# Delta rule's inverse: one whole-array product for two heads, one turn per level, heads kept in their row half

## The chip, the cores and the metric

The kernel runs on one core of a Trainium2 chip as a single launch. The metric is the device time of one execution in microseconds (us). In float32 code each matmul of the program appears in the trace as two matmul records and two weight loads; a transpose through the matrix engine appears as one of each.

## The reference, cut to what matters

The program is a two-layer diffusion block over 256 context and 1024 latent tokens. Its first layer mixes tokens with an mLSTM and an RWKV-7 delta rule. The delta rule is the part of this case:

```python
def rwkv_scan(inputs, S):
    def step(S, xs):
        r, v, kk, w, k, a = xs
        sa = jnp.einsum('bhvk,bhk->bhv', S, -kk)
        S = S * w[:, :, None, :] + sa[..., None] * (kk * a)[:, :, None, :] + v[..., None] * k[:, :, None, :]
        return S, jnp.einsum('bhvk,bhk->bhv', S, r)
```

There are 8 heads of 64 columns, 1280 tokens and two directions. The kernel takes chunks of 64 tokens. Inside a chunk the steps depend on each other through a 64x64 strictly triangular matrix per head, and the chunk is solved with the inverse of (identity minus that matrix). This case is about how the inverse is built.

## The kernel before, in words

The stage is `stage_rwkv_scan` (from line 1540). There are 20 chunks and 2 directions, so 40 scan steps `s`; two steps (two `lane`s) form one batch `b`, and there are B = 20 batches. The 8 heads lie as J = 4 pairs; of pair `j`, head `q` = 0 has rows 0 to 63 and head `q` = 1 has rows 64 to 127. A batch thus has 16 inverses of 64x64.

The inverse is built by doubling. Level 0 is made by GpSimd (`begin_inverse`, line 1990). Then come TOP = 5 levels, n = 1 to 5, so 100 levels in the stage. A level is a chain over three engines:

- `half_product` (line 1833, TensorE) multiplies the strict matrix `strict_t` (the stationary side) with the 32 changed columns of `inv`. There are 16 products with a 64x64 block, and they go over all four combinations of row half and column half of the array (`quarters`).
- `copy_half` (line 1903, ScalarE) copies the result from PSUM into `half`.
- `turn_inverse` (lines 2047 and 2049, VectorE) writes the turned `inv` into `lower`, in three instructions, beside the half product.
- `upper_product` (line 1842, TensorE) multiplies `lower` with `half`: again 16 products of 64x64 over all four combinations.
- `merge_upper` (line 2055, VectorE) writes the result into `inv` under a mask. The next level's half product and turn wait for it.

So that the two products use all four combinations, `inv` stores the heads in two sets: set 0 holds the heads whose inverse lies in its own order and set 1 the others, `own_inverse` finds a head, and the result of a product changes the row half between steps. The PSUM results lie in two banks, `PAIR` and `PAIR + 1` (`pair_bank`, `pair_banks`).

The order on each engine is written out by hand, in the loops over `b` at the end of each engine's block. Between the two products of a level TensorE does work of the batch before (`begin_chunk` 1789, `solve_chunk` 1798, `begin_outputs` 1807, `update` 1815, `end_outputs` 1821) and of the batch ahead (`strict_products` 1732, `products` 1743), and `pull` 1780, `turn_keys` 1755, `turn_v` 1770. VectorE does `read_products` 2039, `add_rest` 2064 and `update_state` 2072 and 2073 between its turns; ScalarE copies `strict_t` (line 1934) and other results. Of these the matrix engine's blocks are: 1732, 1780, 1789, 1798 and 1807 are 64x64; 1743 is 64 rows by 128 columns; 1815 and 1821 are 128 rows by 64 columns; 1755 and 1770 are the whole 128x128. Lines 1732, 1789 and 1798 keep a head in its row half: head 0 uses rows and columns 0 to 63 of the array, head 1 rows and columns 64 to 127.

Of the kernel before, what the change touches and what calls it, by code (L numbers as in the profile page):

```python
# [1539 lines left out]
def stage_rwkv_scan(p, arena, operands, v_dram, shared, spare, own, chunk_decay, y, next_weights, free, bonus_dram):  # L1540
# [30 lines left out]
    strict_read = p.semaphore("r_strict_read")  # L1571
    level0_ready = p.semaphore("r_level0_ready")
# [23 lines left out]
    with ExitStack() as local:  # L1596
# [4 lines left out]
        strict_t = sb("strict_t", [P, 2, 2, J, C])  # L1601
        inv = sb("inv", [P, 2, 2, 2, J // 2, C])
        lower = sb("lower", [P, 2, J, C])
        half = sb("half", [P, 2, J, C // 2])
# [16 lines left out]
        identity = column(0, 5 + R_LEVELS).unsqueeze(1).broadcast_to([P, 2, J // 2, C])  # L1621
# [6 lines left out]
        fours = [(lane, jj) for lane in range(2) for jj in range(J // 2)]  # L1628
        quarters = [(0, 0), (1, 1), (0, 1), (1, 0)]
        four = lambda lane, jj: lane * (J // 2) + jj  # L1630
        own_inverse = lambda b, lane, j, q: inv[part(q), b % 2, (j % 2) ^ q, lane, j // 2, :]
        pair_bank = lambda which, lane, jj: bank(PAIR + which)[:, four(lane, jj) * P:four(lane, jj) * P + C // 2]
        pair_banks = p.psum[:, PAIR:PAIR + 2, :].rearrange("p r (f n) -> p (r f) n", n=P)[:, :, 0:C // 2]
        with nc.Block() as block:
# [88 lines left out]
            def _(pe):  # L1723
# [174 lines left out]
            def _(act):  # L1898
                def copy_half(b, n):
# [3 lines left out]
                    nc.scalar.copy(half[:, :, :, :].rearrange("p q f n -> p (q f) n"), pair_banks).then_inc(half_copied, 1)  # L1903
# [25 lines left out]
                def copy_strict(b, lane):  # L1929
# [4 lines left out]
                    nc.scalar.copy(strict_t[:, b % 2, lane], narrow(bank(STRICT)[:, lane * HALF:(lane + 1) * HALF])).then_inc(strict_read, 1)  # L1934
# [44 lines left out]
            def _(pool):  # L1979
                begun, added = [0], [0]  # L1980

                def begin_inverse(b, lane, q):
# [6 lines left out]
                    pairs = prod[part(q), b % 2, lane, q, :, part(q)].rearrange("p (j r) n -> p r j n", r=2)  # L1989
                    nc.gpsimd.tensor_tensor(inv[part(q), b % 2, :, lane], pairs if q == 0 else pairs[:, ::-1],  # L1990
# [12 lines left out]

                pool.wait_ge(masks_loaded, 16)
# [21 lines left out]
            def _(dve):  # L2026
# [14 lines left out]
                def turn_inverse(b, n):  # L2041
# [4 lines left out]
                    here = inv[:, b % 2].rearrange("p s l j n -> p s (l j) n")  # L2046
# [1909 lines left out]
```

## Time and profile before

| | us |
|---|---|
| median of 3 runs | 2453.71 |
| lowest and highest | 2449.43, 2456.01 |
| the profiled execution | 2456.63 |
| its span | 2454.8 |
| TensorE busy in the span | 2294.7 |
| VectorE busy | 1320.0 |
| ScalarE busy | 794.4 |
| GpSimd busy | 251.0 |

The span is the time between the first and the last instruction; 1.8 us of the execution lie around it. Busy time is the union of an engine's records. The matrix engine has two rows, PE for matmuls and PEld for weight loads, which overlap. PEclk is the clock granted to the matrix engine as a share of 2.4 GHz (0.50 is 1.2 GHz). A line of the timeline merges neighbouring instructions of one group: its first number is when the first began, the second how long until the last ended.

### The profile page before, as it was taken

What the parts mean: (1) busy time and instruction counts of PE and PEld (TensorE: products, weight loads), DVE (VectorE), ACT (ScalarE), POOL (GpSimd) and SP (SyncE); (2) the same over time, 40 slices, a digit from 0 to 9 for tenths busy, and PEclk for the clock granted to TensorE, in tenths of its full rate; (3) what the DMA queues carried; (4) which work ended last, traced back from release to release, by engine and by line L of the source; (5) the groups of instructions that cost most, each with busy time, mean ns of one, the idle gap of its engine ahead of it and who ended that gap; (6) DMA issues with size and microseconds to landing.
All of it is one profiled execution on the core that took longest, in us unless ns stands there. A gap on an engine that the chain in (4) does not pass through costs nothing. (4 is left out here: it accounts for less than half of the span.)

```text
span 2454.8 us, 50670 instructions
## 1 busy us (share of the span) xinstructions
PE 2294.7 (93%) x22140; PEld 1417.6 (58%) x22140; DVE 1320.0 (54%) x2181; ACT 794.4 (32%) x1533; POOL 251.0 (10%) x280
## 2 busy tenths in 40 slices
PE   6999999999989988888887998999998999999898
PEld 4444456666644447887784443444685666756443
DVE  3320335553348756777774454555395666667514
ACT  4121222224455653443232222110101445465411
POOL 0000000000002211111221102341100000000000
PEclk8999999999989998999999998999999999999999
DMA  8100122122056654433325422111122100000233
GB/s 332 60 19 7 43 78 76 63 66 73 19 154 145 172 155 112 118 94 95 90 61 196 138 98 76 47 47 34 69 104 80 36 27 27 28 18 10 96 97 117
DMA packets 131866, 207.29 MB, mean 84 GB/s; under 512 B 15629, under 2 KB 95245, under 8 KB 128062
## 3 DMA queue, kind: packets, MB, share of 16 engines
q1 hardware_dynamic: 118398, 154.74, 20.2%
q0 software_dynamic: 13248, 49.32, 7.0%
q8 instruction: 175, 2.87, 0.5%
q14 instruction: 45, 0.37, 0.1%
HBM read 154.01 MB, written 50.01 MB: 83 GB/s over the span
## 5 line engine op out<-in xcount | busy, mean ns | idle before, releaser
L737 PE MATMUL psum<-arena,shared 128*128 128x512 f32 (+1 forms) x864 | 328.3, 524 | 1.5 <-PEq L223 1.5
L2861 PE MATMUL psum<-arena,second_shared 128*128 128x512 f32 (+1 forms) x640 | 282.3, 568 | 11.1 <-PEq L3682 6.4
L737 PEld LDWEIGHTS psum<-arena,shared 128*128 128x128 f32 x864 | 156.9, 191 | 108.5 <-issue 101.5
L2861 PEld LDWEIGHTS psum<-arena,second_shared 128*128 128x128 f32 x640 | 112.4, 195 | 77.0 <-issue 71.8
L1243 PE MATMUL psum<-shared,arena 128*128 128x512 f32 x320 | 150.0, 618 | 0.0
L2247 PE MATMUL psum<-shared,fin_mix 128*128 128x512 f32 x320 | 143.4, 601 | 2.9 <-POOL fin_mix L2380 2.9
L2247 PEld LDWEIGHTS psum<-shared,fin_mix 128*128 128x128 f32 x320 | 59.8, 192 | 75.0 <-issue 71.5
L1243 PEld LDWEIGHTS psum<-shared,arena 128*128 128x128 f32 x320 | 60.3, 196 | 73.3 <-issue 72.9
L841 ACT ACTIVATE shared<-psum 128x512 f32<-128x512 f32 (+1 forms) x48 | 25.2, 525 | 216.2 <-PE psum L737 216.2
L1842 PE MATMUL psum<-r_half,r_lower 64*64 64x32 f32 x3200 | 78.6, 225 | 13.5 <-issue 11.2
L1903 ACT COPY r_half<-psum 128x256 f32<-128x256 f32 x100 | 37.3, 373 | 162.0 <-PE psum L1833 161.7
L2049 DVE STREAM_TRANSPOSE r_lower<-r_inv 64x256 f32<-64x256 f32 x200 | 87.9, 440 | 2.7
L1990 POOL TENSOR_TENSOR r_inv<-r_prod,shared 64x256 f32<-64x256 f32 x80 | 58.0, 724 | 291.2 <-PE psum L1798 184.2
L1833 PE MATMUL psum<-r_inv,r_strict_t 64*64 64x32 f32 x3200 | 73.9, 225 | 14.6 <-issue 10.9
L330 PE MATMUL psum<-arena,shared 128*128 128x512 f32 (+3 forms) x240 | 87.4, 523 | 0.0
L3146 DVE TENSOR_TENSOR arena<-arena,g_k 128x512 f32<-128x512 f32 x56 | 39.6, 706 | 87.4 <-ACT arena L3014 87.4
L3014 ACT ACTIVATE arena<-arena 128x1024 f32<-128x1024 f32 x64 | 69.4, 1084 | 34.6 <-DVE arena L3127 32.8
L2852 PE MATMUL psum<-second_shared,arena 128*128 128x128 f32 x640 | 80.3, 277 | 0.0
L1833 PEld LDWEIGHTS psum<-r_inv,r_strict_t 64*64 64x64 f32 x3200 | 61.5, 138 | 27.1 <-issue 16.9
L1842 PEld LDWEIGHTS psum<-r_half,r_lower 64*64 64x64 f32 x3200 | 65.9, 139 | 18.7 <-issue 13.0
L2055 DVE COPY_PREDICATED r_inv<-shared,psum 128x256 f32<-128x256 uint32 x100 | 49.6, 496 | 50.2 <-PE psum L1842 49.0
L2852 PEld LDWEIGHTS psum<-second_shared,arena 128*128 128x128 f32 x640 | 75.1, 192 | 1.1 <-issue 0.5
(457 smaller groups left out, 4257.6 us busy)
## 6 DMA issues: line engine op xcount, KB each, us to landing
arena<-scratch_operands SPq DMA_DIRECT2D x152, 128.0 KB, 2.7
shared<-in_l_w_in SPq DMA_DIRECT2D x22, 512.0 KB, 4.0
scratch_spill<-shared POOLq DMA_DIRECT2D x16, 640.0 KB, 3.2
second_shared<-in_l_w_in SPq DMA_DIRECT2D x20, 512.0 KB, 3.9
scratch_operands<-arena POOLq DMA_DIRECT2D x14, 640.0 KB, 8.3
scratch_operands<-arena POOLq DMA_DIRECT2D x28, 320.0 KB, 11.3
shared<-in_l_mod_w SPq DMA_DIRECT2D x8, 1024.0 KB, 9.4
t_matrix<-in_transform SPq DMA_DIRECT2D x8, 1024.0 KB, 4.9
```

The lines of the kernel that those rows point to most:

```text
L330: last = nc.tensor.matmul(p.psum[0:rows_out, bank_of[u], 0:width], lhsT, rhs, start=(k == 0), stop=(k == KT - 1))
L737: last = nc.tensor.matmul(p.psum[:, FILL + f % BANKS, 0:width], weight[:, q % PIECES, k, :], hT[:, k, at:at + width], start=(k == 0), stop ...
L1243: last = nc.tensor.matmul(p.psum[:, PROJECT + u % 2, :], hT[:, k, t * P:(t + 1) * P], weight[:, job, k, :], start=(k == 0), stop=(k == KT ...
L1833: last = nc.tensor.matmul(pair_bank(q, lane, jj)[part(r)], strict_t[part(q), b % 2, lane, 2 * jj + r, :], changed(own_inverse(b, lane, 2 * ...
L1842: last = nc.tensor.matmul(pair_bank(q ^ r, lane, jj)[part(q)], lower[part(r), q ^ r, four(lane, jj), :], half[part(r), q, four(lane, jj), ...
L1990: nc.gpsimd.tensor_tensor(inv[part(q), b % 2, :, lane], pairs if q == 0 else pairs[:, ::-1], identity[part(q)], ALU.add).then_inc(level0_r ...
L2049: last = nc.vector.transpose(lower[part(1 - q), 1], here[part(q), 1])
L2055: nc.vector.copy_predicated(whole[:, :, :, 1 - direction(b)], added_to_pairs(direction(b), n), pair_banks.rearrange("p f (g w) -> p f g w" ...
L2247: last = nc.tensor.matmul(p.psum[:, OUT + 2 * (t % 2) + n, :], mixed[:, t % SLOTS, k, :], weight[:, k, n * BANK:(n + 1) * BANK], start=(k ...
L2852: last = nc.tensor.matmul(bank[:, (t - part[0]) * P:(t - part[0] + 1) * P], hT[:, kk, t * P:(t + 1) * P], w[:, kk, :], start=(kk == 0), st ...
L2861: last = nc.tensor.matmul(bank[:, 0:width], w[:, kk, :], hT[:, kk, first:first + width], start=(kk == 0), stop=(kk == KT - 1))
L3014: nc.scalar.activation(out, out, ACT.Exp).then_inc(sig["exps_ready"], 1)
```

## The change

The strict matrices of the two heads of a pair are stored as one 128x128 block, one head in the upper left, the other in the lower right, with zeros in the other two quarters. The half product of a pair is then one matmul with this whole block (8 per level in place of 16), and each head stays in its own row half. The upper product has as many matmuls as before, but each uses rows and columns of its own half. `inv` has no sets any more, the turn is one VectorE instruction over 512 elements per partition, and both products lie in one PSUM bank. ScalarE copies a strict matrix in two instructions, one per row half. GpSimd clears the zero quarters once, at the start of the stage, in two instructions, and TensorE waits for these before its first product.

```diff
-        strict_t = sb("strict_t", [P, 2, 2, J, C])
-        inv = sb("inv", [P, 2, 2, 2, J // 2, C])
+        strict_t = sb("strict_t", [P, 2, 2, J, P])
+        inv = sb("inv", [P, 2, 2, J, C])
...
+        heads = [(lane, j) for lane in range(2) for j in range(J)]
+        own_inverse = lambda b, lane, j, q: inv[part(q), b % 2, lane, j, :]
+        narrowed = lambda where, lane, j: slice(where * HALF + (lane * J + j) * C // 2, where * HALF + (lane * J + j + 1) * C // 2)
+        products_of = lambda where: bank(PAIR)[:, where * HALF:(where + 1) * HALF]
...
-                    for lane, jj in fours:
-                        for q, r in quarters:
-                            last = nc.tensor.matmul(pair_bank(q, lane, jj)[part(r)], strict_t[part(q), b % 2, lane, 2 * jj + r, :],
-                                                    changed(own_inverse(b, lane, 2 * jj + r, q), direction(b), n), start=True, stop=True)
+                    for lane, j in heads:
+                        last = nc.tensor.matmul(bank(PAIR)[:, narrowed(0, lane, j)], strict_t[:, b % 2, lane, j, :],
+                                                changed(inv[:, b % 2, lane, j, :], direction(b), n), start=True, stop=True)
...
-                    for lane, jj in fours:
-                        for q, r in quarters:
-                            last = nc.tensor.matmul(pair_bank(q ^ r, lane, jj)[part(q)], lower[part(r), q ^ r, four(lane, jj), :],
-                                                    half[part(r), q, four(lane, jj), :], start=True, stop=True)
+                    for lane, j in heads:
+                        for q in range(2):
+                            last = nc.tensor.matmul(bank(PAIR)[part(q), narrowed(1, lane, j)], lower[part(q), lane * J + j, :],
+                                                    half[part(q), lane * J + j, :], start=True, stop=True)
...
+                pe.wait_ge(strict_cleared, 2)
...
-                    nc.scalar.copy(strict_t[:, b % 2, lane], narrow(bank(STRICT)[:, lane * HALF:(lane + 1) * HALF])).then_inc(strict_read, 1)
+                    for q in range(2):
+                        last = nc.scalar.copy(strict_t[part(q), b % 2, lane, :, part(q)],
+                                              narrow(bank(STRICT)[part(q), lane * HALF:(lane + 1) * HALF]))
+                    last.then_inc(strict_read, 1)
...
+                for q in range(2):
+                    blank = strict_t[part(q)].rearrange("p b l j n -> p (b l j) n")[:, :, part(1 - q)]
+                    nc.gpsimd.memset(blank, 0.0).then_inc(strict_cleared, 1)
...
-                    nc.vector.transpose(lower[:, 0], here[:, 0])
-                    for q in range(2):
-                        last = nc.vector.transpose(lower[part(1 - q), 1], here[part(q), 1])
-                    last.then_inc(lower_turned, 1)
+                    nc.vector.transpose(lower[:, :, :].rearrange("p f n -> p (f n)"),
+                                        inv[:, b % 2].rearrange("p l j n -> p (l j n)")).then_inc(lower_turned, 1)
```

## Rows read from the trace of the kernel before

**Rows 1.** Busy time by stretch: the 20 batches; columns as the header says
```profile
core 0: us, PE busy (x) PEld busy (x) DVE busy (x) ACT busy (x) POOL busy (x), PEclk, DMA share, GB/s
925.30:1302.50 377.20, 327.99 (x11490) 302.79 (x11490) 277.32 (x589) 134.03 (x349) 67.43 (x93) 0.97 0.33 89
```

**Rows 2.** Groups of instructions of that stretch: count, busy, mean ns, idle before
```profile
L1842 PE MATMUL psum<-r_half,r_lower 64*64 64x32 f32 x3200 | 78.6, 225 | 13.5 <-issue 11.2 <-DVE r_lower L2049 1.6 <-ACT r_half L1903 0.6
L1833 PE MATMUL psum<-r_inv,r_strict_t 64*64 64x32 f32 x3200 | 73.9, 225 | 14.6 <-issue 10.9 <-DVE r_inv L2055 2.5
...
L1815 PE MATMUL psum<-shared,r_k_tok 128*64 128x64 f32 x384 | 17.7, 232 | 7.4 <-ACT shared L1926 4.1 <-issue 3.3
...
L2049 DVE STREAM_TRANSPOSE r_lower<-r_inv 64x256 f32<-64x256 f32 x200 | 87.9, 440 | 2.7
...
L2055 DVE COPY_PREDICATED r_inv<-shared,psum 128x256 f32<-128x256 uint32 x100 | 49.6, 496 | 50.2 <-PE psum L1842 49.0
L2047 DVE STREAM_TRANSPOSE r_lower<-r_inv 128x256 f32<-128x256 f32 x100 | 44.4, 444 | 12.0 <-POOL r_inv L1990 9.1 <-DVE r_inv L2055 0.5
L1903 ACT COPY r_half<-psum 128x256 f32<-128x256 f32 x100 | 37.3, 373 | 162.0 <-PE psum L1833 161.7
```

**Rows 3.** Timeline of part of a batch: start, us, engine, group, idle before
```profile
1084.11 0.56 PEld L1842 LDWEIGHTS psum<-r_half,r_lower 64*64 64x64 f32 x32
...
1084.71 0.97 PEld L1743 LDWEIGHTS psum<-arena 64*128 64x128 f32 x16
...
1085.80 0.56 PEld L1833 LDWEIGHTS psum<-r_inv,r_strict_t 64*64 64x64 f32 x32
1085.80 0.67 PE L1833 MATMUL psum<-r_inv,r_strict_t 64*64 64x32 f32 x32
1086.26 0.55 PEld L1732 LDWEIGHTS psum<-arena 64*64 64x64 f32 x16
...
1086.73 0.55 PEld L1789 LDWEIGHTS psum<-r_state,arena 64*64 64x64 f32 x16
...
1087.15 0.59 PEld L1842 LDWEIGHTS psum<-r_half,r_lower 64*64 64x64 f32 x31
```

**Rows 4.** Timeline: weight loads of 128x128 blocks, moving 2, 2, 128, 1, 128 columns
```profile
688.32 4.34 PEld L1272 LDWEIGHTS psum<-consts,gp_grown 128*128 128x128 f32 x20 [2.83 <-ACT gp_grown L1361]
...
795.86 2.20 PEld L1272 LDWEIGHTS psum<-consts,gp_grown 128*128 128x128 f32 x19 [0.24 <-issue]
...
1301.95 0.86 PEld L1755 LDWEIGHTS psum<-consts,arena 128*128 128x128 f32 x8
...
1752.76 0.97 PEld L3709 LDWEIGHTS psum<-consts,y_magnitudes 128*128 128x128 f32 x8 [1.12 <-issue]
...
1928.11 3.65 PEld L2852 LDWEIGHTS psum<-second_shared,arena 128*128 128x128 f32 x32
```

**Rows 5.** Timeline of the stage's start, and GpSimd's largest and smallest clearing
```profile
916.97 0.96 PEld L1732 LDWEIGHTS psum<-arena 64*64 64x64 f32 x16 [6.64 <-issue]
...
917.09 0.27 DVE L2076 MEMSET r_state<- 128x256 f32 x1 [8.17 <-PEq L130]
...
L474 POOL MEMSET m_v<- 128x40 f32 x1 | 0.2, 169 | 65.0 <-PE psum L277 65.0
...
L3947 POOL MEMSET const-float32-1.0<- 128x1 f32 x1 | 0.1, 99 | 0.0
```

**Rows 6.** Busy time and granted clock by stretch; columns as in Rows 1
```profile
925.30:945.00 19.70, 16.43 (x421) 15.24 (x421) 11.29 (x24) 4.66 (x12) 2.89 (x4) 0.60 0.25 74
...
936.00:938.00 2.00, 0.67 (x32) 0.56 (x32) 1.97 (x5) 0.37 (x1) 0.72 (x1) 0.87 0.33 88
...
938.00:944.00 6.00, 5.91 (x132) 5.62 (x134) 3.09 (x7) 0.38 (x2) 1.45 (x2) 0.50 0.19 56
...
1305.00:1311.00 6.00, 3.69 (x111) 3.20 (x109) 1.27 (x4) 1.74 (x5) 0.73 (x1) 1.00 0.00 0
```

**Rows 7.** Timeline: a pause inside one group of matmuls
```profile
1116.46 0.64 PE L1842 MATMUL psum<-r_half,r_lower 64*64 64x32 f32 x29
1119.18 0.24 PE L1842 MATMUL psum<-r_half,r_lower 64*64 64x32 f32 x1 [2.09 <-issue]
```

More of the change, by code:

```diff
@@ L1571, in stage_rwkv_scan @@
     strict_read = p.semaphore("r_strict_read")
+    strict_cleared = p.semaphore("r_strict_cleared")
     level0_ready = p.semaphore("r_level0_ready")
@@ L1600, in stage_rwkv_scan @@
         prod = sb("prod", [P, 2, 2, 2, J, 2 * C])
-        strict_t = sb("strict_t", [P, 2, 2, J, C])
-        inv = sb("inv", [P, 2, 2, 2, J // 2, C])
-        lower = sb("lower", [P, 2, J, C])
-        half = sb("half", [P, 2, J, C // 2])
+        strict_t = sb("strict_t", [P, 2, 2, J, P])
+        inv = sb("inv", [P, 2, 2, J, C])
+        lower = sb("lower", [P, 2 * J, C])
+        half = sb("half", [P, 2 * J, C // 2])
         rest, pulled = sb("rest", [P, J, C]), sb("pulled", [P, 2, J, C])
@@ L1620, in stage_rwkv_scan @@
             [P, 2 * J, C >> (n + 1), 1 << n])
-        identity = column(0, 5 + R_LEVELS).unsqueeze(1).broadcast_to([P, 2, J // 2, C])
+        identity = column(0, 5 + R_LEVELS).broadcast_to([P, J, C])
         PAIR, KEYS, TURN, STRICT, CHAIN, OUT = 0, (2, 5), 3, 5, 6, 7
@@ L1627, in stage_rwkv_scan @@
         flat = lambda a: a.rearrange("p l j n -> p (l j) n")
[L1628 to L1633, printed above, removed]
+        heads = [(lane, j) for lane in range(2) for j in range(J)]
+        own_inverse = lambda b, lane, j, q: inv[part(q), b % 2, lane, j, :]
+        narrowed = lambda where, lane, j: slice(where * HALF + (lane * J + j) * C // 2, where * HALF + (lane * J + j + 1) * C // 2)
+        products_of = lambda where: bank(PAIR)[:, where * HALF:(where + 1) * HALF]
         with nc.Block() as block:
@@ L1902, in copy_half @@
                         act.wait_ge(upper_ready, TOP * b + n - 1)
-                    nc.scalar.copy(half[:, :, :, :].rearrange("p q f n -> p (q f) n"), pair_banks).then_inc(half_copied, 1)
+                    nc.scalar.copy(half[:, :, :].rearrange("p f n -> p (f n)"), products_of(0)).then_inc(half_copied, 1)
                 def copy_keys(b, lane):
@@ L1988, in begin_inverse @@
                     begun[0] += 1
-                    pairs = prod[part(q), b % 2, lane, q, :, part(q)].rearrange("p (j r) n -> p r j n", r=2)
-                    nc.gpsimd.tensor_tensor(inv[part(q), b % 2, :, lane], pairs if q == 0 else pairs[:, ::-1],
+                    nc.gpsimd.tensor_tensor(inv[part(q), b % 2, lane], prod[part(q), b % 2, lane, q, :, part(q)],
                                             identity[part(q)], ALU.add).then_inc(level0_ready, 1)
@@ L2045, in turn_inverse @@
                         dve.wait_ge(upper_merged, TOP * b + n - 1)
-                    here = inv[:, b % 2].rearrange("p s l j n -> p s (l j) n")
-                    nc.vector.transpose(lower[:, 0], here[:, 0])
-                    for q in range(2):
-                        last = nc.vector.transpose(lower[part(1 - q), 1], here[part(q), 1])
-                    last.then_inc(lower_turned, 1)
+                    nc.vector.transpose(lower[:, :, :].rearrange("p f n -> p (f n)"),
+                                        inv[:, b % 2].rearrange("p l j n -> p (l j n)")).then_inc(lower_turned, 1)
                 def merge_upper(b, n):
                     dve.wait_ge(upper_ready, TOP * b + n)
-                    whole = inv[:, b % 2].rearrange("p s l j (g t w) -> p (s l j) g t w", t=2, w=1 << n)
+                    whole = inv[:, b % 2].rearrange("p l j (g t w) -> p (l j) g t w", t=2, w=1 << n)
                     nc.vector.copy_predicated(whole[:, :, :, 1 - direction(b)], added_to_pairs(direction(b), n),
-                                              pair_banks.rearrange("p f (g w) -> p f g w", w=1 << n)).then_inc(upper_merged, 1)
+                                              products_of(1).rearrange("p (f g w) -> p f g w", g=C >> (n + 1), w=1 << n)).then_inc(upper_merged, 1)
                 def add_rest(b, lane):
```

## The prediction

> **What bounds the kernel now.** I read the busy time of the stage first [rows 1]. In the 377.2 us of the 20 batches TensorE is busy 328.0 us (87%), VectorE 277.3, ScalarE 134.0. TensorE is idle for 49.2 us, 2.5 us of a batch's 18.9. Second the groups with their idle time [rows 2]. VectorE waits 49.0 us for the upper product and ScalarE 161.7 us for the half product: both follow TensorE. TensorE in turn waits little for them: 1.6 us for the turn at line 2049, 2.5 for the merge, 0.6 for the copied half product, 4.1 at line 1815 for ScalarE's copy. Most of its idle time in these rows is "issue" (11.2, 10.9, 3.3 us), time in which it waited for nothing visible. A case of it: a group of 32 pauses 2.09 us before its last matmul, where no semaphore stands [rows 7]. So the bound is TensorE's own work, in the order written out, and what the change is worth is read from how long TensorE needs for each group.
>
> Third the timeline, for that length: the distance from the first weight load of a group to the first of the next [rows 3]. The half product with 32 instructions (two for each of 16 matmuls) goes from 1085.80 to 1086.26: 0.46 us, or 14 ns an instruction. The strict products, 16 instructions that use only row half q with column half q, go from 1086.26 to 1086.73: 0.47 us, 29 ns each. So do those of line 1789: 0.42 us, 26 ns each. Equal blocks cost twice as much when only two of the four array quarters take turns: a quarter takes a new 64x64 block each 55 ns in all three.
>
> **The half product.** 8 matmuls with a 128x128 block are 16 instructions per level, in place of 32. No group of before has such a block with 32 moving columns; the nearest on both sides are 1 or 2 columns and 128 columns [rows 4]. At the full clock, 19 loads with 2 moving columns take 2.20 us; less the 0.19 of the last one, 18 distances, 0.112 us each. 8 loads with 1 column: (0.97 - 0.19)/7 = 0.111. 32 loads with 128 columns: (3.65 - 0.19)/31 = 0.112. The three agree, so 32 columns get 0.112 too. The group takes 16 x 0.112 = 1.79 us in place of 0.46: +1.33 us per level, **+133 us** over 100 levels. The block is twice as wide for the load, and the four quarters no longer work beside each other; half of what it loads is zeros.
>
> The Trainium skill, "TensorE: Matmul & The Clock Gate", section "Part 3: Packing small matmuls — row/col tiling", says in "The mechanism" that a weight load overlaps with running matmuls only when the row group differs. By that rule the 32 columns would come on top of each load (with 0.112/4 = 0.028 us as an estimate of them), and the half products would cost another 45 us. The row with 128 moving columns speaks against it: they fit wholly within the load's 0.112 us.
>
> **The upper product** keeps its 32 instructions but uses only the two diagonal quarters, as lines 1732 and 1789 do. 32 of them cost 0.47 + 0.42 = 0.89 us in place of 0.46 [rows 3]: **+43 us** over 100 levels. Bounds: 2 x 0.42 and 2 x 0.47, so +38 to +48.
>
> **Changes of the block's shape.** Where the next group has another shape the distance is longer: upper product to line 1743 is 1084.11 to 1084.71, 0.60 in place of 0.46, so 0.14 us [rows 3]. The half product now has a shape that its neighbours lack. At n = 1 this replaces a change that is there already (the turned keys before it are 128x128); in the other four levels one change is new, at the entry or at the exit. 4 x 20 x 0.14 = **+11 us**; bounds 0 and twice that.
>
> **VectorE's turn** falls from 0.444 + 2 x 0.440 = 1.32 us to one instruction of 512 elements. Bounds: 0.44 as for 256 elements, 0.90 as for twice that; I take 0.7. It saves 0.6 us of VectorE per level but stands beside the half product and the copy, and TensorE waits for it 1.6 us in all. The merge has the same 256 elements, the level 0 sum the same 64x256: nothing.
>
> **ScalarE** copies a strict matrix in two instructions. Bounds for the second are nothing, if it is as short as its share, and another 0.37; 40 times, at most 15 us on an engine with 243 us idle. At n = 4 the copy stands before the half product's copy; TensorE then does update and outputs of the batch before, 32 instructions, some 0.9 us at 26 to 29 ns each. Nothing.
>
> **The wait for the cleared quarters** stands before TensorE's first product. That product begins at 916.97 us as the stage opens, so the wait is on the path: all products, and with them ScalarE, VectorE and GpSimd, are behind it. Each of two instructions clears 64 partitions x 1024 elements. GpSimd took 169 ns for 40 elements and 99 for 1, 1.8 ns per element, so up to 1.9 us each; VectorE took 0.27 us for 256, so about 1.1 each at its rate [rows 5]. **+3 us**; bounds 0.2 and 5.
>
> **Slow clock.** The first stretch of the stage runs at a granted 0.60 on average [rows 6], with about five of the first levels at 0.50 (1.2 GHz), where a 128x128 load takes 4.34 us / 20 = 0.22 us [rows 4]. The extra of a level is 1.33 + 0.43 + 0.11 = 1.87 us at full clock and twice that here: 5 x 1.9, or **+8 us** with some of it lost in idle time. Bounds 0 and 15.
>
> **Idle time that goes.** With 1.9 us more per level on TensorE, results of the others come early in its order. The chain of a level is the half product to the end of its last matmul (15 x 0.112 + 0.23 = 1.9), the copy 0.37, the upper product (31 x 0.028 + 0.23 = 1.1), the merge 0.50 [rows 2], and four hand-overs of some 0.1 us (an estimate): 4.3 us, 21 per batch. TensorE's work is longer: 18.9 - 2.5 idle + 5 x 1.87 = 25.8 us per batch. So VectorE and ScalarE aren't the bound, and the 8.8 us of named waits in [rows 2] go. The unnamed pauses come in dense streams of short instructions [rows 7]; the half product has half as many, spread over four times the time, and I let most of them go too. Of 49.2 us idle I take back **-35 us**; bounds 0 and -49.
>
> Sum: 133 + 43 + 11 + 3 + 8 - 35 = +163 us on the profiled execution of 2456.6 (span 2454.8 and 1.8 around it): 2619.6. The median of the runs shown is 2.9 below that execution, so I predict 2617 us. Of this stage, 377 us become about 537, 26.9 us per batch.
>
> **Rivals.**
> A. *Instructions are what costs.* If an instruction costs 14 ns whatever its block, as within the groups of before, the half product falls to 16 x 14 = 0.23 us (-23 us), the upper product stays at 0.46, and with +11 for shapes, +3 for clearing and -4 for the turn's waits it comes to 2453.7 - 13 = 2441 us. It decides once a 128x128 block loads in less than 0.46/16 = 0.029 us with the upper product unchanged. For it: 32 instructions fit in 0.46 us. Against: the three groups with whole blocks, all at 0.11, and the diagonal groups at twice the price per instruction. The Trainium skill's "TensorEngine Tiling (Array Packing)", section "Instruction Overhead", has a rule of this kind: some 60 cycles per matmul, and one free column costs as much as 60. By that figure 16 fewer instructions are an estimated 0.4 us less per level. The rows have 14 ns per instruction where that is 25, and 112 where the block is whole, so neither the charge nor the gain is seen.
>
> B. *The clock falls.* In the half product few columns move for 1.8 us. The clock fell to 0.50 after two microseconds with only 0.67 us busy, and stayed there for 6 us though TensorE was then busy [rows 6]. If every half product ran slow, each would cost 0.11 x 16 = 1.7 us more: +170, 2787 us. Against it: at the stage's end, with 3.69 us busy in 6, the clock stayed at 1.00, and with the change TensorE has fewer pauses than before.
>
> C. *The diagonal price is that of the columns.* Lines 1732 and 1789 move 64 columns, the upper product 32. If the columns set their pace, the upper product keeps 0.46 us: 43 us less, 2574. Against: the quarter's 55 ns per block is the same with 32 columns at line 1842 as with 64.
>
> **How the numbers follow.** Forecast 0.82 (slower), B 0.08 (slower), C 0.04 (slower), A 0.04 (faster), and 0.02 that gains and losses cancel. The forecast's own ends: 8 turned keys, single-instruction transposes with 128x128 blocks, load in 0.86 us [rows 4], so (0.86 - 0.14)/7 = 0.103 us apart (0.14 for the last); at that price the half products cost 16 x 0.103 - 0.46 = 1.19 us more, +119. With 38, 0, 0.2, 0 and -49 for the other terms this is +108, 2562. All high: 133 + 48 + 22 + 5 + 15 and nothing recovered: +223, 2677. The range of 2562 to 2675 holds the forecast and C and leaves out A and B, 0.14 with the gap between. A change within 0.3% (7.4 us) is what a measurement of this kernel can't tell from none; faster 0.04, same 0.02, slower 0.94.
>
> **What would show it.** Line 1833's group: 1600 instructions in place of 3200, on 128x128 blocks, weight loads 0.112 us apart, 1.8 us to the next group. The upper product: 0.89 us to the next. ScalarE's and VectorE's waits for TensorE grow, TensorE's for them are under 3 us in all; its busy share of the stage is above 93%. One turn of about 0.7 us per level. First product 2 to 4 us after the stage opens. I would be wrong in the main term if whole blocks came less than 0.1 us apart; in the recovery, if TensorE still idles 40 us or more; and in the clock, if the granted mean of the stage is below 0.9.

## The result, and the profile after

The changed kernel takes 2584.1 us (median; 2580.8 to 2587.7) against 2453.7 for the kernel before. The ratio is 1.053, with an interval of 1.051 to 1.055: slower by 130 us. The forecast was 2617, so the direction was right and the size 33 us too high. The profiled execution took 2587.7 us with a span of 2585.9, 131.1 more than the span of before.

First the busy time by stretch, as in [rows 1]: the whole of the 20 batches, then four pieces from their beginning and their end.

```profile
core 0: us, PE busy (x) PEld busy (x) DVE busy (x) ACT busy (x) POOL busy (x), PEclk, DMA share, GB/s
929.90:1437.70 507.80, 503.42 (x9893) 484.33 (x9892) 211.98 (x389) 149.46 (x388) 67.18 (x93) 0.94 0.24 66
929.90:949.90 20.00, 18.62 (x169) 17.96 (x170) 3.90 (x6) 3.41 (x10) 0.72 (x1) 0.50 0.11 31
965.00:969.00 4.00, 4.00 (x53) 3.94 (x50) 1.16 (x2) 1.45 (x3) 0.00 (x0) 0.50 0.25 78
969.00:973.00 4.00, 4.00 (x73) 3.96 (x71) 0.42 (x1) 1.41 (x4) 0.00 (x0) 0.88 0.27 72
1417.00:1421.00 4.00, 4.00 (x83) 3.94 (x84) 1.02 (x3) 0.65 (x2) 0.73 (x1) 0.52 0.02 4
```

The stage went from 377.2 to 507.8 us, +130.6. The wait at its start adds 2.0, and the rest of the program is 1.5 shorter: the whole difference lies in this stage. It has 1597 matmul records fewer and TensorE is idle for 4.4 us in place of 49.2. The granted clock is 0.50 until about 970 us and again from 1417 us to the end of the 20 batches.

Second the groups with their idle time, as in [rows 2].

```profile
L1831 PE MATMUL psum<-r_inv,r_strict_t 128*128 128x32 f32 x1600 | 207.3, 286 | 3.3 <-DVE r_inv L2056 2.4
L1840 PE MATMUL psum<-r_half,r_lower 64*64 64x32 f32 x3200 | 116.7, 225 | 1.1 <-ACT r_half L1902 1.1
L2050 DVE STREAM_TRANSPOSE r_lower<-r_inv 128x512 f32<-128x512 f32 x100 | 71.0, 710 | 5.1 <-POOL r_inv L1991 1.0
L2056 DVE COPY_PREDICATED r_inv<-shared,psum 128x256 f32<-128x256 uint32 x100 | 49.4, 494 | 130.7 <-PE psum L1840 130.7
L1902 ACT COPY r_half<-psum 128x256 f32<-128x256 f32 x100 | 37.2, 372 | 259.8 <-PE psum L1831 259.8
```

The 11 us of "issue" before each of TensorE's two products are gone, and the other engines wait longer: VectorE's merge 130.7 us in place of 49.0, ScalarE's copy 259.8 in place of 161.7.

Third the timeline of weight loads at the full clock, as in [rows 3].

```profile
1170.43 1.86 PEld L1831 LDWEIGHTS psum<-r_inv,r_strict_t 128*128 128x128 f32 x16 [0.18 <-DVE r_inv L2056]
1172.34 0.55 PEld L1814 LDWEIGHTS psum<-r_uv,r_k_tok 128*64 128x64 f32 x16
...
1173.42 1.01 PEld L1840 LDWEIGHTS psum<-r_half,r_lower 64*64 64x64 f32 x32
1174.47 0.97 PEld L1742 LDWEIGHTS psum<-arena 64*128 64x128 f32 x16
1175.56 1.86 PEld L1831 LDWEIGHTS psum<-r_inv,r_strict_t 128*128 128x128 f32 x16
1177.46 0.54 PEld L1731 LDWEIGHTS psum<-arena 64*64 64x64 f32 x16
```

The half product goes from 1175.56 to 1177.46, 1.90 us; its loads are (1.86 - 0.19)/15 = 0.111 us apart. The upper product takes 1.05 us to a group of another shape and, as the shortest distance in the stage, 0.93 to one of its own. The half product of 1170.43 comes again at 1194.51, so a batch takes 24.1 us; it took 18.9 before.

The stage's start, as in [rows 5]:

```profile
919.70 1.94 POOL L2007 MEMSET r_strict_t<- 64x1024 f32 x2 [4.17 <-POOLq L130]
919.82 0.27 DVE L2077 MEMSET r_state<- 128x256 f32 x1 [8.16 <-PEq L130]
921.70 0.93 PEld L1731 LDWEIGHTS psum<-arena 64*64 64x64 f32 x16 [8.62 <-POOL r_strict_t L2007]
```

TensorE's first load comes 2.0 us after the other engines have begun; before, it came 0.12 us ahead of VectorE's clearing.

### The profile page after: what moved, and what is told of

The parts are those of the page before. It is cut to its first block and busy times, and to the rows that moved or that the text cites. A ratio compares the mean times of both kernels' runs of the same rounds, so it can differ in the third digit from the quotient of the medians.

```text
span 2585.9 us, 47313 instructions
## 1 busy us (share of the span) xinstructions
PE 2465.8 (95%) x20540; PEld 1596.7 (62%) x20540; DVE 1254.4 (49%) x1981; ACT 809.1 (31%) x1573; POOL 252.2 (10%) x282
## 3 DMA queue, kind: packets, MB, share of 16 engines
q1 hardware_dynamic: 118398, 154.74, 19.2%
q8 instruction: 163, 2.67, 0.4%
## 5 line engine op out<-in xcount | busy, mean ns | idle before, releaser
L2862 PE MATMUL psum<-arena,second_shared 128*128 128x512 f32 (+1 forms) x640 | 282.5, 568 | 10.9 <-PEq L3683 6.4
L1831 PE MATMUL psum<-r_inv,r_strict_t 128*128 128x32 f32 x1600 | 207.3, 286 | 3.3 <-DVE r_inv L2056 2.4
L1831 PEld LDWEIGHTS psum<-r_inv,r_strict_t 128*128 128x128 f32 x1600 | 198.2, 202 | 13.1 <-DVE r_inv L2056 6.4
L1902 ACT COPY r_half<-psum 128x256 f32<-128x256 f32 x100 | 37.2, 372 | 259.8 <-PE psum L1831 259.8
L1840 PE MATMUL psum<-r_half,r_lower 64*64 64x32 f32 x3200 | 116.7, 225 | 1.1 <-ACT r_half L1902 1.1
L2056 DVE COPY_PREDICATED r_inv<-shared,psum 128x256 f32<-128x256 uint32 x100 | 49.4, 494 | 130.7 <-PE psum L1840 130.7
L1840 PEld LDWEIGHTS psum<-r_half,r_lower 64*64 64x64 f32 x3200 | 107.7, 142 | 4.0 <-issue 1.3
L3433 PE MATMUL psum<-arena,yf_weight 128*128 128x512 f32 x168 | 74.4, 592 | 0.0
## 6 DMA issues: line engine op xcount, KB each, us to landing
scratch_operands<-arena POOLq DMA_DIRECT2D x28, 320.0 KB, 10.9
```

The lines of the kernel that those rows point to most:

```text
L1831: last = nc.tensor.matmul(bank(PAIR)[:, narrowed(0, lane, j)], strict_t[:, b % 2, lane, j, :], changed(inv[:, b % 2, lane, j, :], directio ...
L1840: last = nc.tensor.matmul(bank(PAIR)[part(q), narrowed(1, lane, j)], lower[part(q), lane * J + j, :], half[part(q), lane * J + j, :], star ...
L2862: last = nc.tensor.matmul(bank[:, 0:width], w[:, kk, :], hT[:, kk, first:first + width], start=(kk == 0), stop=(kk == KT - 1))
L3433: last = nc.tensor.matmul(bank(made), left[:, k, :], right[:, k, :], start=(k == 0), stop=(k == HALF - 1))
```

## What TensorE's pauses of before were

The prediction did not explain the "issue" pauses and took back 35 us of idle time. Both questions, why so much came back and why it had been idle, lead to one place. The weight loads of a later batch of the kernel before, from one pause to the next:

```profile
1101.81 0.13 PEld L1815 LDWEIGHTS psum<-r_uv,r_k_tok 128*64 128x64 f32 x1 [0.51 <-issue]
1101.83 0.13 PEld L1821 LDWEIGHTS psum<-r_uv,r_prod 128*64 128x64 f32 x1
1101.87 0.14 PEld L1815 LDWEIGHTS psum<-r_uv,r_k_tok 128*64 128x64 f32 x1
1101.88 0.59 PEld L1821 LDWEIGHTS psum<-r_uv,r_prod 128*64 128x64 f32 x15
1102.54 0.56 PEld L1842 LDWEIGHTS psum<-r_half,r_lower 64*64 64x64 f32 x32
1103.14 0.97 PEld L1743 LDWEIGHTS psum<-arena 64*128 64x128 f32 x16
1104.23 0.56 PEld L1833 LDWEIGHTS psum<-r_inv,r_strict_t 64*64 64x64 f32 x32
1104.69 0.55 PEld L1732 LDWEIGHTS psum<-arena 64*64 64x64 f32 x16
1105.16 0.43 PEld L1789 LDWEIGHTS psum<-r_state,arena 64*64 64x64 f32 x12
1105.79 0.20 PEld L1789 LDWEIGHTS psum<-r_state,arena 64*64 64x64 f32 x4 [0.20 <-issue]
```

Both pauses stand inside a group, where no semaphore is. Between them are 1+1+1+15+32+16+32+16+12 = 126 loads, each with its matmul: 252 instructions, in 3.98 us. The stage's 11490 loads make 91 such stretches; at 4.0 us each that is 365 us, and the stage without its slow-clock share is 364.7 us long. The page gives the size that fits: the queue named "instruction" (q8) moved 163 packets of 16.4 KB (2.67 MB) in the kernel after and 175 (2.87 MB) in the one before, 12 fewer, where 1600 loads and 1600 matmuls fewer are 12.5 blocks of 256.

I call this theory **supply**: instructions reach TensorE in blocks of 256, and dense short matmuls outrun that. By it, the kernel before was bound mostly by the number of its instructions, and the one after by its array work, since 9892 loads need only 78.5 x 4.0 = 314 us. The **rival** is that the pauses are chance gaps or hidden hand-overs, so that array work counts in both kernels.

The times of the DMA packets in the same trace decide it. In the stage of before, q8 fetched 91 packets of 16384 bytes. Of all pauses of at least 0.12 us in the weight loads' row 47 stand between two loads of one line, and 43 of these end 1.2 to 1.7 us after a packet of q8 has landed; only 12% of the stage's time lies in that window. From one of the 43 to the next there are 125 to 127 loads or a multiple of that (252 or 253, 379 or 380, and so on), never another number. Where it is one stretch (17 cases), it takes 3.9 to 4.6 us, 4.03 in the middle. In the stage of after q8 fetched 79 packets, and no such pause stands between two loads of one line.

The same times say what the 4.0 us consist of. A packet takes 1.1 us (0.9 to 1.7), TensorE goes on 1.4 us after its landing, and in 33 of the 47 cases the next packet starts 1.0 to 1.4 us after TensorE went on: some 3.7 us for one round. So most of the round is not the transfer. What the two waits beside it consist of stays open.

Under the Trainium skill's "Runtime: NRT & Kernel Launch", section "Instruction fetch mechanics", the instruction memory is refilled in 16 KiB blocks of 256 instructions, and crossing a block is mostly hidden because instructions are dispatched more slowly than blocks come. The block's size agrees with the 16384 bytes and the 252 (the other instructions of a block are waits and the like); that it is hidden doesn't agree with pauses of 0.2 to 2 us here.

In the experiments "full-clock length" is the stage's length less half the time that it ran at a granted 0.50, summed over 4 us pieces of the view by stretch. The stage lasts from the first half product to the first product behind the last batch, for the kernel before 0.5 us longer than the stretch of [rows 1]:

```
kernel           stage   at 0.50   full-clock length   time, us   ratio to before
before           377.7     26.0        364.7            2453.7      1
after            507.8     60.6        477.6            2584.1      1.051 to 1.055
e1_diagonal      409.4     29.8        394.5            2486.7      1.009 to 1.015
e2_all_columns   501.9     40.4        481.7            2581.8      1.049 to 1.054
e3_three_turns   500.1     42.8        478.7            2584.1      1.050 to 1.055
b1_tiny          416.8     49.8        391.8            2504.3      1.015 to 1.020
b2_merged        384.9     17.0        376.4            2470.6      1.004 to 1.008
b3_interleaved   384.1     39.7        364.3            2460.2      0.999 to 1.002
a3_interleaved   556.5    170.7        471.2            2642.2      1.068 to 1.077
a3_again         572.9    207.1        469.3            2652.4      1.076 to 1.083
a4_columns       505.1     47.8        481.2            2583.3      1.048 to 1.052
```

Each ratio is to runs of the kernel before on the same chip (medians of 2452 to 2461 us).

## Experiments

**e1_diagonal**: the kernel after, with each whole block as its two 64x64 quarters.

```diff
-                        last = nc.tensor.matmul(bank(PAIR)[:, narrowed(0, lane, j)], strict_t[:, b % 2, lane, j, :],
-                                                changed(inv[:, b % 2, lane, j, :], direction(b), n), start=True, stop=True)
+                        for q in range(2):
+                            last = nc.tensor.matmul(bank(PAIR)[part(q), narrowed(0, lane, j)], strict_t[part(q), b % 2, lane, j, part(q)],
+                                                    changed(inv[part(q), b % 2, lane, j, :], direction(b), n), start=True, stop=True)
```

> The changed kernel with one edit: the half product of a pair is two 64x64 products again, each on its own row half and column half (16 matmuls, 32 instructions per level), in place of one with the 128x128 block. TensorE's instruction count per level is then that of the kernel before. Pure work of a batch, from the distances of groups: 24.1 us in the changed kernel less 5 x (1.90 - 0.93) = 19.2 us. Theory (supply): in the kernel before TensorE was held not by its matmuls but by how fast its instructions come, some 4.0 us for each stretch of about 126 weight loads and 126 matmuls, 18.6 us per batch; its pauses stand at these boundaries. So 19.2 us of work nearly covers the supply, the pauses all but vanish, and the total is 2465 to 2485 us. Rival (whole-block price alone, pauses belong to the instruction count and stay): 2454 + 5 x 0.9 x 20 = 2544 us.

2486.7 us, 1.7 above the range that supply gave and far under the rival's 2544. The stage and the two products:

```profile
927.70:1337.10 409.40, 403.26 (x11493) 382.81 (x11492) 213.74 (x389) 149.39 (x388) 67.40 (x93) 0.96 0.30 82
```

```profile
L1832 PE MATMUL psum<-r_inv,r_strict_t 64*64 64x32 f32 x3200 | 116.6, 224 | 3.6 <-DVE r_inv L2057 2.4 <-issue 0.5
L1841 PE MATMUL psum<-r_half,r_lower 64*64 64x32 f32 x3200 | 115.1, 222 | 2.2 <-ACT r_half L1903 1.1 <-issue 1.0
```

It has the 11492 loads of the kernel before, and both products on two quarters of the array. Two products at 0.93 in place of 0.46 us are +94 us of array work over 100 levels, yet the full-clock length grows by only 29.8: the other 64 filled the pauses. The "issue" before the two products fell from 22.1 to 1.5 us, and the stage takes 394.5/91.2 = 4.3 us per 126 loads, above supply's 4.0: array work, by the expectation's sum 19.2 us per batch, is now the larger of the two. So of the change's 130 us about 97 are the whole block and 33 the rest: the diagonal layout, with the 2 us of the clearing.

**b1_tiny**: the kernel before, with 8 matmuls of one column added at every level. Nothing reads their results.

```diff
+                    for spot in range(2):
+                        for q, r in quarters:
+                            nc.tensor.matmul(bank(PAIR + q)[part(r), spot * P + C:spot * P + C + 1], p.const("ident")[part(q), part(r)],
+                                             p.const("ones")[part(q), 0:1], start=True, stop=True)
```

> The kernel before with 8 tiny matmuls added at the head of each half product: 64x64 constants as the block, one moving column, results into unused columns of the same two banks (nothing reads them). They are 16 weight loads and 16 matmuls more per level, at 14 ns a pair 0.23 us of array work. Theory (supply, 4.0 us for each 126 weight loads and 126 matmuls): 1600 pairs more are 12.7 such stretches, +51 us, 2500 us, and the pauses stay at distances of about 126 loads. Rival (TensorE is held by the array's work and by pauses that do not follow the count): at most 0.23 x 100 = 23 us, 2475 us, less what falls into idle time.

2504.3 us, 1.5 to 2.0% over the kernel before. Weight loads between two pauses:

```profile
1104.81 0.97 PEld L1743 LDWEIGHTS psum<-arena 64*128 64x128 f32 x15 [0.26 <-issue]
1105.90 0.32 PEld L1833 LDWEIGHTS psum<-consts 64*64 64x64 f32 x16
1106.12 0.56 PEld L1837 LDWEIGHTS psum<-r_inv,r_strict_t 64*64 64x64 f32 x32
...
1109.07 0.43 PEld L1807 LDWEIGHTS psum<-r_state,arena 64*64 64x64 f32 x12 [1.00 <-issue]
1109.80 0.34 PEld L1833 LDWEIGHTS psum<-consts 64*64 64x64 f32 x16
...
1113.03 0.20 PEld L1846 LDWEIGHTS psum<-r_half,r_lower 64*64 64x64 f32 x7 [0.64 <-issue]
```

A row of 16 tiny loads takes 0.22 us of the array, 22 us over 100 levels, and TensorE had 49 us of idle time to put them in. The stage grew by 39.1 us instead, and the pauses inside a group still come every 126 loads or so (127 from 1104.81 to 1109.07, 126 from there to 1113.03). But 12 of the 39.1 are slow clock, and the full-clock length grew by 27, between supply's 51 and the rival's 23 at most. With 13085 loads that is 3.8 us per 126, so 4.0 is not a fixed price. The size alone does not decide; the packets do: q8 fetched 104 in this stage, 13 more, and 58 of 60 pauses between two loads of one line end 1.2 to 1.7 us after a landing.

**b3_interleaved** and **a3_interleaved**: in the kernel before and in the kernel after, the products of `solve_chunk` and `begin_outputs`, which each use two quarters, are issued alternately, so that all four quarters take turns.

```diff
-                        solve_chunk(b - 1, 0)
-                        begin_outputs(b - 1, 0)
+                        solve_and_begin_outputs(b - 1, 0)
```

> The kernel before with the matmuls of the solve (row half q to column half q) and of the begun outputs (row half q to column half 1-q) issued alternately instead of one group after the other, so that all four array quarters take turns: the same instructions, and the pair of groups should take some 0.5 us in place of 0.9. Theory (supply): the instructions come no faster, so the total is the same within 4 us, 2452, with longer pauses elsewhere. Rival (the array's work is the bound): 0.4 us x 38 less, 2437 us.

> The same edit in the changed kernel, whose instructions come faster than its 24.1 us of work per batch need them. Theory (supply in the kernel before, array's work in the changed one): here the 0.4 us x 38 do count, 2584 - 15 = 2569 us. Rival (alternating gains nothing, or TensorE's work is not the bound here either): 2584 us; then the other run with this edit says nothing of the supply.

The 32 loads of an alternated group come within some 0.5 us, where lines 1807 and 1798 of before took 0.8 (1087.6 to 1088.4): 0.3 us less array work, 40 times. In the kernel before that gave nothing: 0.999 to 1.002, full-clock length 364.3 against 364.7. Against runs of before on the same chip (2458.7 us) it took 1.5 us more, where supply expected none and the rival 15 less: the rival is out. In the kernel after the full-clock length did fall, by 6.4 us, but the time rose to 2642: a clear miss. The stage ran at 0.50 for 171 us in place of 61. Run again, it took 2652 us with 207 us at 0.50:

> The alternated kernel once more, beside the one with 64 moving columns, on the same chip. If the order itself makes the clock fall, it takes 2620 to 2650 us again with over 120 us of the stage at a granted 0.50; if the first time was a disturbance of that chip or hour, it takes 2565 to 2580 with 60 us or less.

So it is the order and no accident. In nearly every batch of it stands a wait of 0.47 us for the merge before the half product of n = 2 (0.18 in the kernel after), which the shorter groups no longer cover. From a3_again:

```profile
1060.79 0.14 PEld L1809 LDWEIGHTS psum<-r_rest,r_inv 64*64 64x64 f32 x2
1061.40 1.86 PEld L1846 LDWEIGHTS psum<-r_inv,r_strict_t 128*128 128x128 f32 x16 [0.47 <-DVE r_inv L2069]
1063.30 0.69 PEld L1829 LDWEIGHTS psum<-shared,r_k_tok 128*64 128x64 f32 x16
1063.86 0.99 PEld L1835 LDWEIGHTS psum<-shared,r_prod 128*64 128x64 f32 x16
```

The 16 loads at line 1829 begin fast and end slow (0.69 us where 0.55 is usual), and those at 1835 are slow. From there the clock stays low for 30 us though TensorE is never idle (other falls last 14 or 30), as the stretches of the same execution show:

```profile
1063.50:1067.50 4.00, 4.00 (x70) 3.82 (x68) 1.38 (x4) 1.75 (x5) 0.00 (x0) 0.52 0.31 78
1071.50:1091.50 20.00, 20.00 (x254) 19.28 (x254) 5.34 (x10) 2.86 (x8) 2.89 (x4) 0.50 0.17 43
1091.50:1095.50 4.00, 4.00 (x50) 3.94 (x44) 1.15 (x2) 1.76 (x3) 0.00 (x0) 0.64 0.24 66
```

Not every such wait brings a fall: of 19 in a3_interleaved five were followed within 2.2 us by one, of 19 in a3_again seven. The kernel after has one fall late in the stage, after a wait of 0.64 us at 1415.48, again with the first half product behind it:

```profile
1415.48 2.00 PEld L1831 LDWEIGHTS psum<-r_inv,r_strict_t 128*128 128x128 f32 x16 [0.64 <-DVE r_inv L2056]
1417.54 0.93 PEld L1788 LDWEIGHTS psum<-r_state,arena 64*64 64x64 f32 x16
```

**e2_all_columns** and **a4_columns**: the half product moves all 64 columns of `inv`, of which the copy takes the 32 that are wanted; first in the kernel after, then in a3_interleaved. The diff leaves out the copy and the upper product's move to the second bank.

```diff
-                        last = nc.tensor.matmul(bank(PAIR)[:, narrowed(0, lane, j)], strict_t[:, b % 2, lane, j, :],
-                                                changed(inv[:, b % 2, lane, j, :], direction(b), n), start=True, stop=True)
+                        last = nc.tensor.matmul(bank(PAIR)[:, at(lane, j)], strict_t[:, b % 2, lane, j, :],
+                                                inv[:, b % 2, lane, j, :], start=True, stop=True)
...
```

> The changed kernel, but the half product with the 128x128 block moves all 64 columns of an inverse instead of the 32 changed ones (results in their own bank; the copy takes the changed 32). Both theories agree that a group stays at 1.9 us at full clock, since 128 moving columns fit in the load's 0.112 us. Theory (columns hold the clock): the half product moves few columns, and the 60 us that the changed kernel's stage spends at 1.2 GHz, against 26 before, come from that; with twice the columns the slow time falls to 30 us or less and the total to 2560 to 2570 us. Rival (the clock does not follow the columns moved): slow time 50 to 65 us, total 2580 to 2590.

> The kernel after with both edits: solve and begun outputs alternated between the four quarters, and half products that move all 64 columns of the inverse in place of 32. The alternated kernel alone took 2642 us, and 171 us of its stage ran at a granted 0.50. If the columns moved during the whole-block products hold the clock up, the slow-clock time falls to 60 us or less and the time to about 2575 us. If it is the length of the whole-block products or their waits that let the clock fall, whatever moves in them, the slow-clock time stays above 120 us and the time stays at 2625 to 2655.

In the kernel after, 64 columns change nothing that can be told: 2581.8 us, as the rival expected. The 40 us at 0.50, against 61 in the kernel after, lie between the two expectations and show nothing, since e3 with 32 columns had 43: in both the late fall is missing or short. Twice the columns cost next to nothing (1.93 us to the next group in place of 1.90), as each load takes 0.11 us anyway:

```profile
L1831 PEld LDWEIGHTS psum<-r_inv,r_strict_t 128*128 128x128 f32 x1600 | 194.7, 199 | 13.3 <-DVE r_inv L2057 6.4 <-issue 1.0
```

In the alternated kernel they took 59 to 69 us off: 2583.3 us, and 48 us at 0.50 in place of 171 and 207. It has the same 19 waits, and none of them is followed by a fall:

```profile
1063.00:1083.00 20.00, 19.63 (x422) 18.62 (x421) 9.58 (x18) 6.43 (x18) 1.84 (x3) 1.00 0.27 68
```

```profile
1111.35 1.87 PEld L1846 LDWEIGHTS psum<-r_inv,r_strict_t 128*128 128x128 f32 x16
1116.17 1.86 PEld L1846 LDWEIGHTS psum<-r_inv,r_strict_t 128*128 128x128 f32 x16 [0.47 <-DVE r_inv L2070]
```

So in mid-stage the moved columns made the difference, at equal waits, and the longer wait did at equal columns (no fall there in the kernel after). But 64 columns don't always hold the clock. After the 0.64 us wait near the stage's end it fell in a4_columns too:

```profile
1411.82 1.98 PEld L1846 LDWEIGHTS psum<-r_inv,r_strict_t 128*128 128x128 f32 x16 [0.64 <-DVE r_inv L2070]
1413.91 0.93 PEld L1788 LDWEIGHTS psum<-r_state,arena 64*64 64x64 f32 x16
```

```profile
1413.50:1433.50 20.00, 19.47 (x249) 18.68 (x249) 3.99 (x8) 2.78 (x8) 0.73 (x1) 0.50 0.01 2
```

With 32 columns it fell there in the kernel after and in e4, in e3 only after the second such wait, and in e2 with 64 columns after neither. What decides between them stays open. So does the slow stretch at the stage's start, some 27 to 41 us with 32 and with 64 columns; e1, which has no whole block, has 30 us of it too, so the whole blocks are not its condition. The expected 2575 us was missed by 8: the full-clock length did not fall.

**e3_three_turns**: the kernel after, with the turn in three instructions as before (256, 256 and 256 elements).

```diff
-                    nc.vector.transpose(lower[:, :, :].rearrange("p f n -> p (f n)"),
-                                        inv[:, b % 2].rearrange("p l j n -> p (l j n)")).then_inc(lower_turned, 1)
+                    nc.vector.transpose(lower[:, 0:J, :].rearrange("p f n -> p (f n)"), inv[:, b % 2, 0].rearrange("p j n -> p (j n)"))
+                    for q in range(2):
+                        last = nc.vector.transpose(lower[part(q), J:2 * J, :].rearrange("p f n -> p (f n)"),
+                                                   inv[part(q), b % 2, 1].rearrange("p j n -> p (j n)"))
+                    last.then_inc(lower_turned, 1)
```

> The changed kernel with VectorE's turn in three instructions again (one of 128x256, two of 64x256), 1.3 us in place of 0.71 us per level. Theory (the turn is beside TensorE's work): TensorE does 1.9 us of half product and 0.9 us or more of other groups before it needs the turned inverse, so the total is the same, 2584 within 4 us. Rival (the single turn is worth what it saves and the change would have been slower without it): up to 0.6 x 100 = 60 us more, 2644.

2584.1 us against 2584.1. The 0.57 us per level that VectorE saves (1.28 against 0.71) are wholly hidden.

**e4_late_wait**: the wait for the cleared quarters stands before the first half product. One execution.

```diff
+                    if b == 0 and n == 1:
+                        pe.wait_ge(strict_cleared, 2)
...
-                pe.wait_ge(strict_cleared, 2)
```

> The changed kernel with TensorE's wait for the cleared quarters moved from before its first product to before its first half product. Theory: the first product begins within 0.1 us of the stage's opening instead of 2.0 us after it, and the first half product 2.0 us earlier relative to the opening; 2582 us. Rival (something else, as the loads of operands, holds the first product too): no change in the distance.

```profile
919.99 1.95 POOL L2008 MEMSET r_strict_t<- 64x1024 f32 x2 [4.17 <-POOLq L130]
920.00 0.96 PEld L1731 LDWEIGHTS psum<-arena 64*64 64x64 f32 x16 [6.64 <-issue]
```

TensorE starts with GpSimd and the 2.0 us go; the total of 2585.4 can't show them.

**b2_merged**: the kernel before, with state update and end of outputs as one product with a 128x128 block. That takes 640 loads from lines 1815 and 1821 and adds 160 in which an identity matrix places the state in PSUM. VectorE's addition goes, and ScalarE copies keys and outputs in two instructions each, at other places in its order. The diff shows the one product alone.

```diff
-                        last = nc.tensor.matmul(bank(OUT)[part(1 - q), at(0, j)], prod[:, b % 2, lane, q, j, part(1 - q)],
-                                                uv(2 * b + lane)[:, q, j, :], start=False, stop=(j == J - 1))
+                        last = nc.tensor.matmul(bank(OUT)[:, at(q, j)], prod[:, b % 2, lane, q, j, :],
+                                                uv(s)[:, q, j, :], start=False, stop=(j == J - 1 and q == 1))
...
```

> The kernel before with fewer but dearer matmuls: state update and outputs of a chunk become one product with a 128x128 block (the turned keys are copied into the free half of the masked products, so 8 matmuls in place of 16), and the old state is placed in PSUM by two matmuls with the identity in place of VectorE's addition. Per chunk 64 instructions become 40, while the array's work grows by 1.79 - 0.92 + 0.4 = 1.3 us. Theory (supply): 480 weight loads fewer are 3.8 stretches of 4.0 us, -15 us, and some 3 us come back in the last two chunks, which have nothing beside them: 2440 us (2435 to 2450), faster than both kernels. Rival (the array's work is the bound): 2.6 us more in each of 20 batches, +52 us, 2504 us.

2470.6 us: slower, between the two theories, so supply's forecast of a gain was missed.

```profile
L1823 PE MATMUL psum<-shared,r_prod 128*128 128x64 f32 x416 | 52.2, 279 | 4.3 <-ACT shared L1930 3.7 <-issue 0.5
...
L1835 PE MATMUL psum<-r_inv,r_strict_t 64*64 64x32 f32 x3200 | 75.6, 223 | 13.6 <-issue 6.2 <-POOL r_inv L1997 4.1 <-DVE r_inv L2062 3.0
```

"Issue" before the half product fell from 10.9 to 6.2 us, but named waits for GpSimd, VectorE and ScalarE took its place. With TensorE's array work, now larger, and these chains, a batch needs 18.8 us at the full clock, more than the 17.5 that its 11037 loads give at 4.0 us per 126. It seems that the removed instructions were worth something only until the next limit, and that was close; which of the edit's parts costs the rest isn't shown. No version tried beats the kernel before.

## Why the prediction was right, and where its size was off

The terms by the prediction's own steps, beside what the traces give:

```
                           predicted   measured
half product                  +133       +144    1.90 - 0.46, with the shape change at its exit
upper product                  +43        +47    0.93 - 0.46
changes of shape               +11        in the two above
wait for the clearing           +3         +2    921.70 against 919.70
slow clock                      +8        +17    (60.6 - 26.0)/2
idle time that goes            -35        -78    what is left of the stage's +130.1 (507.8 - 377.7)
sum                           +163       +132    131.1 between the spans
```

**The mechanism held.** The price of a whole block, 0.112 us, read from blocks with 1, 2 and 128 moving columns [rows 4], is what 32 and 64 columns pay. The diagonal price per quarter [rows 3] held too; rival C is out, since the upper product with 32 columns takes 0.93 us as two groups with 64 do. Rival A falls by the same two numbers. With the shape changes the three product terms are 187 us predicted and 191 measured.

**The mis-sized term is the idle time.** It was put at -35 with -49 as its end. TensorE's idle time did fall by 45 us, but that counts only what shows as idle. A pause after a short matmul is partly covered by the matmul's own record, 0.22 us long where the next could start after 0.014 to 0.028. The weight loads' row, whose records are shorter, lost 51 us of idle (74.4 to 23.5). And from the distances of groups, array work grew by 191 us at the full clock and the full-clock length by 113, from which the 78 follow. The step that was off is "of 49.2 us idle I take back 35", and with it the 18.9 - 2.5 = 16.4 us taken as TensorE's work in a batch. The bound should have been the array work of a batch, not the idle time. Adding up the shortest distance of each pair of neighbouring groups gives 14.5 to 15.0 us per batch of before, and 24.0 to 24.5 of after, 9.5 more, which over 20 batches is the 191 of the terms again. A batch of before takes some 4 us more than its sum, one of after at the full clock less than 0.1: these 4 us were there to be filled. Supply says why they were empty, and why all of them went: by it the stage of after needs 314 us, far under its 478. The pauses that end behind a landing, in a group or between two, are 41 us of the 78 as the weight loads' row shows them; the others are waits for engines or covered by other records, and no run splits them further. e1 and b3 show the same from both sides; b1's and b2's sizes fit it only in part.

**The slow clock** was put at +8, with about five levels at 0.50. It cost 17: the first stretch lasted 40 us, and a second of 20 came near the end. Some of this is chance: e3, with the same half product, spent 43 us at 0.50 and not 61. Rival B ("the clock falls") was priced as if every half product ran slow, and that did not come. Its mechanism is real, though: with a wait of 0.47 us per batch in place of 0.18 the stage ran slow for 171 to 207 us. The argument used against it, that fewer pauses protect the clock, is borne out by a3 beside the kernel after; a4 has the pauses of a3 and keeps its clock in mid-stage, so they don't decide alone. The kernel after stands close to that edge.

**The edits put at nothing** were worth nothing: the turn (e3), and, without a run of its own, ScalarE's second copy of a strict matrix, which takes 0.37 us beside TensorE's work.

One sum of the prediction is a little off: its high terms add up to 2677 us, and its range ends at 2675. Nothing rests on that.

## What to carry to other kernels

Price an edit to dense small matmuls twice: by array time, with each block's shape and which quarters work beside each other, and by the number of instructions; the time lies near the larger of the two sums (within 8% in the kernels here), and most of the difference is what an edit may fill or free. Pauses inside a group of matmuls where no semaphore stands, at equal counts of instructions and at an equal time after a packet of the instruction queue has landed, are the mark of the second. A whole 128x128 block is no merger of four quarters: in float32 with few moving columns it cost 0.112 us where four-quarter use put a 64x64 block in every 0.014, so one that is half zeros doubles the work and then some.

## What the runs showed of the hardware

- Dense short matmuls waited for their instructions: blocks of 16384 bytes, with 126 loads and 126 matmuls each, came one per 4.0 us in the kernel before (91 packets; 43 of 47 pauses inside a group end 1.2 to 1.7 us after a landing). The transfer is 1.1 us of it; why the next one starts so late isn't settled. With tiny matmuls added (b1_tiny) it was 3.8 us.
- Loads of 128x128 float32 blocks follow each other every 0.111 to 0.112 us with 1, 2, 32, 64 and 128 moving columns. The Trainium skill's "TensorE: Matmul & The Clock Gate", section "Part 3: Packing small matmuls — row/col tiling", lets a load overlap with running matmuls only when the row group differs; here they overlap with the same row group, as 32 and 64 columns take the same 1.9 us and 128 columns don't lengthen the distance of two loads.
- After waits of 0.47 us before whole blocks with 32 moving columns the granted clock fell to 0.50 in 5 and 7 of 19 cases, for some 14 or 30 us with TensorE busy throughout (a3_interleaved, a3_again); with 64 moving columns in none of 19 (a4_columns). The columns that were moved for nothing saved 59 to 69 us. After a wait of 0.64 us it fell with either width (kernel after, a4_columns), and in e2_all_columns not.
